# The feed-forward part of a decoder step in two phases: inner features through DRAM, down projection with seven products

## The chip, the cores and the metric

The kernel is one program on one core of a Trainium2 chip. The metric is the device time of that core in microseconds. Three runs of the kernel before took 2767.11, 2770.23 and 2770.42 us; the median is 2770.23 us. All data is float32; the matmuls read float32r operands.

## The reference, cut to what matters

The program is one step of a one-layer hybrid decoder for 512 prompt tokens and 8 sample tokens (520 columns, in two halves of 260). Projections, four mixers and cross attention come first and are not touched. The change lies in the last lines of the layer:

```python
D_MODEL = 2048; D_FF = 4 * D_MODEL

xm = rmsnorm(h, p['norm_mlp_g'])
h = h + jnp.square(jax.nn.relu(xm @ p['w_up'])) @ p['w_down']
...
y = RMSNorm_final(h)
```

## The kernel before, in words

Everything is kept transposed: features on the 128 partitions, the 520 tokens along the columns. Each float32 operand is split into a high part (rounded to float32r) and a low part (the rest), and each product of 128x128 weights by 260 columns is three matmuls: high by high, high by low, low by high. For weights, ScalarE makes the high part `whi` by a copy of 128x1024, and VectorE makes the low part `wlo` by a subtraction. Four slots of each are in use, so a part can be made up to four units ahead of TensorE.

The 8192 inner features are done in 8 chunks of 8 tiles (KF = 8). Chunk 0 takes its up projection as plain tiles (`up_tile`, `up_low`). In that stage VectorE also forms sums of the four quarters of the moving operand (two feature halves by two token halves, `sums_of`, `sums_low` into `th`, `tl`). The other chunks use these sums for a seven-product form of a 2x2 block multiplication (Strassen's, in Winograd's form): a quad is two output tiles of 128 features, computed by seven products of 24 matmuls instead of eight.

A quad needs four pieces of `w_up` (A11, A22, A21, A12, 512 KB each, in the ring RAW4) and sums of them. S1 = A21 + A22 is not made by VectorE: SP loads A21's columns a second time into `sums` and GpSimd issues an adding DMA S1 += A22 (line 947). S2 = S1 - A11, A21 := A11 - A21 and S2 := A12 - S2 are VectorE operations (`sum_of`, k = 2, 3, 4: lines 3058, 3061, 3065). The order by which VectorE works is written out by hand in `quad`. The load of S1 for the next quad waits for the low part of the fifth product, which reads S1:

```python
sp.wait_ge(s.s_sum, 2 * KF + 3 * Q - 2)
sp.wait_ge(s.w_lo, product_of(*((c, q - 1) if q else (c - 1, QUADS - 1)), 4) + 1)
sp.dma_start(S1.rearrange("p (k n) -> p k n", n=P),
             kp(io["w_up"])[:, 0:KF, col:col + P]).then_inc(s.glu_in, 16)
```

Results of the products are combined by VectorE and ScalarE into `c1` and `c2t`, then come relu and square, and the split into `fh` and `fl` (`hidden_even`, `hidden_odd`).

After each chunk's up projection comes its part of the down projection: 16 output tiles of 48 matmuls (`down_part`, line 2259). For each tile VectorE multiplies the PSUM tile by rB, the inverse root mean square (line 3146), and adds it to the residual tile `hr`, which ScalarE's queue loads from `hscr` in DRAM and stores back (line 3150). In the last chunk the sum goes to `hF`, and squares are gathered for the final norm.

Of the kernel before, what the change touches and what calls it, by code (L numbers as in the profile page):

```python
# [21 lines left out]
P = 128  # L22
# [34 lines left out]
U_DOWN = 4 * (T_MLP + QUADS)  # L57
PRODUCTS = 7
U_CHUNK = PRODUCTS * QUADS + KT
SLOT = (0, 1, 2, 3, 0, 1, 3)  # L60

O_KV, O_OUT, O_Q, O_O, O_MLP = 30, 38, 54, 70, 86
O_DOWN = O_MLP + KF


def unit_of(c, n):

    return U_DOWN + U_CHUNK * c + n


def product_of(c, q, s):

    return U_DOWN + KT + U_CHUNK * (c - 1) + PRODUCTS * q + s


def group_of(c, g):

    return g if c == 0 else (QUADS + 4) * c - 4 + g


def quad_of(c, q):

    return QUADS * (c - 1) + q
# [7 lines left out]
HID_ORDER = (range(KF), (1, 0, 3, 2, 5, 4, 7, 6))  # L91
# [80 lines left out]
def build(nc, io, consts_ap, outs):  # L172
# [8 lines left out]
    dscr = nc.dram_tensor("dscr", [128], F32, kind="Internal").ap()  # L181
    hscr = nc.dram_tensor("hscr", [P, KT, TOK], F32, kind="Internal").ap()
# [22 lines left out]
    with ctx:  # L205
# [19 lines left out]
        fh = at("fh", [P, KF, TOK], R_H, F32R)  # L225
        fl = at("fl", [P, KF, TOK], R_H + LO // 2, F32R)
# [4 lines left out]
        hF = at("hF", [P, KT, TOK], R_B)  # L231
        raw2 = at("raw2", [P, 2, 1024], R_A + KT * HALF * 4)
        sums = at("sums", [P, 2, 1024], R_A + LO + KT * HALF * 4)
# [97 lines left out]
        ynat = at("ynat", [P, 5, D], R_A)  # L331
# [53 lines left out]
        part = at("part", [P, TOK], FFN)  # L385
        hr = at("hr", [P, 4, TOK], FFN + 3168)
        msum = at("msum", [P, 2, 2, HALF], FFN + 3168)
        tsum = at("tsum", [P, 4, HALF], FFN + 3168 + 4160)
        rF = at("rF", [P, 8], R_S + 1024)
# [180 lines left out]
        s.hid_hi = sem("hid_hi")  # L570
# [5 lines left out]
        s.h_add = sem("h_add")  # L576
# [29 lines left out]
        def halves(t):  # L606
# [5 lines left out]
        hr_in, HR_IN = (s.h_in, s.kh_in, s.vh_in), (48, 64, 64)  # L612
        hr_st, HR_ST = (s.xs_st, s.ys_st), (64 + 16 * KT, 576)
# [9 lines left out]
                 (mh[:, 1, KF:KT, :], ml[:, 1, KF:KT, :]))  # L623

# [59 lines left out]
        def _(sp):  # L684
# [142 lines left out]
            def load_quad(c, q):  # L827

                for r, (i, j) in enumerate(((0, 0), (1, 1), (1, 0), (0, 1))):
                    if q == 0:  # L830
                        n = unit_of(c - 1, KT - 4 + r)
                        sp.wait_ge(s.w_hi, n + 1)
# [7 lines left out]
                    if r == 2:  # L840
                        Q = quad_of(c, q)
                        if Q > 0:
                            sp.wait_ge(s.s_sum, 2 * KF + 3 * Q - 2)
                            sp.wait_ge(s.w_lo, product_of(*((c, q - 1) if q else (c - 1, QUADS - 1)), 4) + 1)
# [2397 lines left out]
```

## Time and profile before

| | |
|---|---|
| median of 3 runs | 2770.23 us (2767.11 to 2770.42) |
| the profiled execution, whole time | 2766.59 us |
| its span | 2764.8 us |
| TensorE busy | 2731.3 us, 99% |
| VectorE busy | 1513.4 us, 55% |
| ScalarE busy | 910.8 us, 33% |
| GpSimd busy | 618.6 us, 22%, none of it arithmetic in the feed-forward part |
| DMA | 428.92 MB, 155 GB/s over the span |

The busy time of an engine is the union of its instructions' spans. Matmuls overlap in the rows: one is shown with 0.28 us, though one starts each 0.12 us. The time from start to start is what counts for a sum. The same holds for VectorE: an operation of 1024 columns shows 1.22 us, and the next starts 1.14 us after it. The granted clock of TensorE was 0.992 on average.

### The profile page before, as it was taken

To read this page: it belongs to the slowest core of one execution; us is meant where nothing else is said; L and a number is where in the kernel's file an instruction comes from. 1 tells how busy PE (TensorE), PEld (TensorE's weight loads), DVE (VectorE), ACT (ScalarE), POOL (GpSimd) and SP (SyncE) were. 2 spreads that over 40 slices of the span, in tenths; PEclk is the share of its full clock that TensorE was granted. 3 is DMA by queue.
4 is the path that set the end of the run, shared out by engine and by line. 5 is a ranking of instruction groups with operands and counts; after the bars stand their busy time and mean duration, and the time that the engine had idled before them with its cause. 6 is when DMAs were issued, how large, how long until landed. Compare 5 with 4: busy or idle time off the path is not lost.

```text
span 2764.8 us, 51075 instructions
## 1 busy us (share of the span) xinstructions
PE 2731.3 (99%) x21572; PEld 2616.8 (95%) x21572; DVE 1513.4 (55%) x2063; ACT 910.8 (33%) x1187; POOL 618.6 (22%) x292
## 2 busy tenths in 40 slices
PE   9999999999999999999999999999999999999998
PEld 7999998777999988789999999999999999999998
DVE  4687936666323334422474655746557465564665
ACT  5221125535222211222332432514325143251442
POOL 2545434675443322344200000000000000000000
PEclk9999999999999999999999999999999999999999
DMA  6734345555532666543327666666665665656653
GB/s 191 142 101 103 103 129 163 169 176 162 169 91 76 206 198 198 161 133 114 109 83 215 166 173 181 159 187 165 173 180 157 191 162 170 179 157 197 162 143 109
DMA packets 576409, 428.92 MB, mean 155 GB/s; under 512 B 36041, under 2 KB 493615, under 8 KB 574767
## 3 DMA queue, kind: packets, MB, share of 16 engines
q1 hardware_dynamic: 500152, 308.70, 38.8%
q10 hardware_dynamic: 72027, 102.69, 12.3%
q0 software_dynamic: 4032, 14.68, 2.8%
q8 instruction: 149, 2.44, 0.4%
q14 instruction: 49, 0.40, 0.0%
HBM read 357.78 MB, written 53.84 MB: 149 GB/s over the span
## 4 chain that ended last, share of the span: by engine, by line
PE 86%; issue 6%; POOL 4%; DVE 2%; ACT 1%; DMA 1%; SPq 0%; POOLq 0%; DVEq 0%; ACTq 0%
PE lin L1654 32%; PE lin L2259 27%; PE aux L2224 17%; PE lin L2224 3%; POOL wlo L932 3%; POOL wlo L890 2%; PE aux L1976 1%; PE aux L1931 1%; PE lin L1871 1%; PE aux L1922 1%; PE lin L1744 1%; DVE rot L2311 0%; PE aux L1821 0%; PE aux L1817 0%; DMA piece<-in_cache_mem_v 0%
## 5 line engine op out<-in xcount | busy, mean ns | idle before, releaser
L890 POOL TENSOR_TENSOR wlo<-raw,whi 128x1024 fp32r<-128x1024 f32 x176 | 433.6, 2467 | 658.9 <-ACT whi L976 467.3
L2259 PE MATMUL lin<-fl,whi 128*128 128x260 f32 x2048 | 577.3, 282 | 0.0
L2259 PE MATMUL lin<-fh,wlo 128*128 128x260 f32 x2048 | 577.2, 282 | 0.0
L2259 PE MATMUL lin<-fh,whi 128*128 128x260 f32 x2048 | 576.8, 282 | 0.0
L1486 ACT ACTIVATE whi<-raw 128x1024 fp32r<-128x1024 f32 x212 | 224.2, 1057 | 507.6 <-DVE hr L3150 400.1
L2259 PEld LDWEIGHTS lin<-fh,wlo 128*128 128x128 f32 x2048 | 385.8, 188 | 0.0
L2259 PEld LDWEIGHTS lin<-fh,whi 128*128 128x128 f32 x2048 | 385.2, 188 | 0.0
L2259 PEld LDWEIGHTS lin<-fl,whi 128*128 128x128 f32 x2048 | 384.9, 188 | 0.0
L3041 DVE TENSOR_TENSOR wlo<-raw,whi 128x1024 fp32r<-128x1024 f32 x240 | 292.6, 1219 | 29.8 <-ACT whi L1486 29.8
L947 POOL DMA_DIRECT2D sums<-raw x28 | 24.4, 871 | 1242.8 <-DMA sums<-in_w_up 1242.8
L3146 DVE TENSOR_TENSOR part<-lin,rB 128x520 f32<-128x520 f32 x128 | 89.5, 699 | 383.0 <-PE lin L2259 376.5
L976 ACT ACTIVATE whi<-raw 128x1024 fp32r<-128x1024 f32 x140 | 147.7, 1058 | 452.6 <-PE lin L1654 324.9
L1654 PE MATMUL lin<-xh,whi 128*128 128x260 f32 x896 | 257.3, 287 | 0.0
L1654 PE MATMUL lin<-xl,whi 128*128 128x260 f32 x896 | 254.5, 284 | 0.0
L1654 PE MATMUL lin<-xh,wlo 128*128 128x260 f32 x896 | 254.2, 284 | 0.0
L2224 PE MATMUL aux<-th,wlo 128*128 128x260 f32 x672 | 189.8, 282 | 0.0
L2224 PE MATMUL aux<-th,whi 128*128 128x260 f32 x672 | 189.7, 282 | 0.0
L2224 PE MATMUL aux<-mh,wlo 128*128 128x260 f32 x672 | 189.7, 282 | 0.0
L2224 PE MATMUL aux<-ml,whi 128*128 128x260 f32 x672 | 189.7, 282 | 0.0
L2224 PE MATMUL aux<-mh,whi 128*128 128x260 f32 x672 | 189.7, 282 | 0.0
L2224 PE MATMUL aux<-tl,whi 128*128 128x260 f32 x672 | 189.6, 282 | 0.0
L1654 PEld LDWEIGHTS lin<-xh,whi 128*128 128x128 f32 x896 | 170.2, 190 | 2.5 <-issue 1.7
(483 smaller groups left out, 6836.4 us busy)
## 6 DMA issues: line engine op xcount, KB each, us to landing
raw<-in_w_up SPq DMA_DIRECT2D x128, 512.0 KB, 4.4
raw<-in_w_down SPq DMA_DIRECT2D x128, 512.0 KB, 4.3
hr<-hscr ACTq DMA_DIRECT2D x128, 260.0 KB, 3.4
raw<-in_w_in SPq DMA_DIRECT2D x60, 512.0 KB, 3.8
hscr<-hr ACTq DMA_DIRECT2D x112, 260.0 KB, 2.1
raw<-in_w_out SPq DMA_DIRECT2D x32, 512.0 KB, 3.9
raw<-in_w_q SPq DMA_DIRECT2D x32, 512.0 KB, 4.0
piece<-in_cache_mem_k SPq DMA_DIRECT2D x32, 512.0 KB, 6.0
```

The costliest lines, as they stand in the source:

```text
L890: pool.tensor_tensor(wlo[:, slot, :], raw[:, slot % 2, :], whi[:, slot, :].bitcast(F32), ALU.subtract).then_inc(s.w_lo, 1)
L932: pool.tensor_tensor(wlo[:, slot, :], src, whi[:, slot, :].bitcast(F32), ALU.subtract).then_inc(s.w_lo, 1)
L976: act.activation(whi[:, slot, :], raw[:, slot % 2, :], ACT.Copy).then_inc(s.w_hi, 1)
L1486: act.activation(whi[:, slot, :], src, ACT.Copy).then_inc(s.w_hi, 1)
L1654: mm = pe.matmul(lin[:, 2 * i + f, 0:HALF], w, x, start=(n == 0 and part == 0), stop=(n == KT - 1 and part == 2))
L1744: mm = pe.matmul(lin[:, 2 * i + f, 0:HALF], w, m[:, kk, HALF * f:HALF * f + HALF], start=(kk == 0 and part == 0), stop=(kk == KT - 1 and p ...
L1871: mm = pe.matmul(lin[:, 2 * i + f, 0:HALF], w, m[:, k, HALF * f:HALF * f + HALF], start=(k == 0 and part == 0), stop=(k == KT - 1 and part ...
L1922: mm = pe.matmul(aux[32 * j:32 * j + 32, 2, :], pTd[:, m, 32 * b:32 * b + 32], piece[:, j, m, :], start=(g == 0 and m == 0), stop=(g == 1 ...
L2224: mm = pe.matmul(out, w, m[:, kk, :], start=(first and kk == 0 and part == 0), stop=(last and kk == KF - 1 and part == 2), skip_group_chec ...
L2259: mm = pe.matmul(lin[:, 2 * i + f, 0:HALF], w, x[:, kk, HALF * f:HALF * f + HALF], start=(first and m == 0 and part == 0), stop=(last and ...
L3041: v.tensor_tensor(wlo[:, slot, :], src, whi[:, slot, :].bitcast(F32), ALU.subtract).then_inc(s.w_lo, 1)
L3146: v.tensor_tensor(halves(part[:]), lin_tile(n % 2), halves(rB[:]), ALU.mult).then_inc(s.tile_free, 1)
```

## The change

Phase 1 computes the up projection of all eight chunks without a break: four pairs of plain tiles, then 28 quads. rB, which before was applied after the down projection, is applied to the squared features. From each quad of feature tiles (two of an even, two of an odd tile's halves) VectorE forms the four sums that the seven-product form of the down projection wants (`hidden_sums`), and ScalarE's queue stores the seven blocks to a new DRAM tensor `hidd` by two DMAs per quad (`store`).

Phase 2 goes through the chunks again. SP loads a chunk's seven blocks (`load_block`, 532 KB each) into one of two sets, ScalarE and VectorE split each into its high and low part (`block_hi`, `block_lo`). The 16 output tiles of a chunk are 4 groups of 4 tiles; a group is seven products of 24 matmuls, on A11, A22, A21, A12 of `w_down` and four sums, now all made by VectorE (`down_sum`). ScalarE copies the PSUM pair X three times (`copied`), VectorE adds four corners into `cbuf`, and GpSimd's queue adds `cbuf` onto the residual `hscr` in DRAM by an adding DMA, except in the last chunk, where `hscr` is loaded into `hF` and VectorE adds.

```diff
+    hidd = nc.dram_tensor("hidd", [N_CHUNK, P, 7, 4, HALF], F32, kind="Internal").ap()
 # GpSimd's queue
-            for c in range(1, N_CHUNK):
-                for u in range(QUADS):
+            for Q in range(N_QUAD):
...
+            for G in range(N_GROUP - GROUPS):
+                g = G % GROUPS
+                pool.wait_ge(s.c_done, C_DONE + 4 * G + 4)
+                pool.dma_start(hscr[:, 4 * g:4 * g + 4, :], cbuf[G % 2][:], accum_op=ALU.add, max_dma_last_dim=4160).then_inc(c_add[G % 2], 16)
 # ScalarE
-                act.activation(fh[:, tile, :], buf, ACT.Copy).then_inc(s.hid_hi, 1)
+            def store(R):
+                c, kk = R // QUADS, R % QUADS
+                act.wait_ge(s.t_done, T_DONE + R + 1)
+                dma(hidd[c, :, 0, kk, :], st[:, R % 2, 0, :], st_out[R % 2])
+                dma(hidd[c, :, 1:7, kk, :], st[:, R % 2, 2:8, :], st_out[R % 2])
+            def quad(Q):
...
                 for k in (4, 5, 6):
-                    hi_product(c, q, k)
+                    hi_up(Q, k)
+                store(QUADS + Q - 1)
 # TensorE
-            down(0, HID_ORDER[0])
-            for c in range(1, N_CHUNK):
-                for u in range(QUADS):
-                    quad(c, u)
-                down(c, HID_ORDER[1])
+            def down_product(G, k, first, last):
+                n, p = down_n(G, k), G // GROUPS
+                pe.wait_ge(s.w_lo, n + 1)
+                if G % GROUPS == 0:
+                    pe.wait_ge(s.blk_lo, BLK_LO + 7 * p + k + 1)
+                hi, lo = xbh[p % 2][k], xbl[p % 2][k]
+                for pr in range(2):
+                    for kk in range(4):
...
+            def group(G):
+                if G > 0:
+                    pe.wait_ge(s.copied, COPIED + 3 * G)
+                down_product(G, 0, True, True)
+                if G > 0:
+                    pe.wait_ge(s.c_done, C_DONE + 4 * G)
...
+                down_product(G, 1, True, True)
...
+            for Q in range(N_QUAD):
+                quad(Q)
+            for G in range(N_GROUP):
+                group(G)
 # VectorE
+            def hidden_sums(R):
+                b = st[:, R % 2, :, :]
+                tt(b[:, 4:6, :], b[:, 1:4:2, :], b[:, 0:2, :], ALU.subtract)
+                tt(b[:, 6, :], b[:, 3, :], b[:, 4, :], ALU.subtract)
+                tt(b[:, 7, :], b[:, 6, :], b[:, 2, :], ALU.subtract, s.t_done)
+            def even(Q):
+                v.wait_ge(s.up_sq, act_n(Q, 6))
+                v.tensor_tensor(st[:, Q % 2, 0:2, :], halves(c1[:]), halves(rB[:]), ALU.mult).then_inc(s.hid_lo, 1)
+                v.wait_ge(s.hid_lo, KF + 2 * Q + 2)
+                hidden_sums(QUADS + Q)
...
             for p in range(QUADS):
...
+                if p == 0:
+                    inverse(6, D, 2)
+                up_scaled(p, 0)
...
-                if p == 0:
-                    inverse(6, D, 2)
...
+                v.wait_ge(s.hid_lo, 2 * p + 2)
+                hidden_sums(p)
+            up_sum(0, 2)
+            for Q in range(N_QUAD):
+                quad(Q)
+                if Q == N_QUAD - 2:
+                    block_lo(0)
+                    block_lo(1)
```

The order on VectorE in the middle of a quad, before: from S2 (`sums<-sums,raw`) to the low part of the fifth product (the third `wlo<-sums` or, counted with raw, the fourth `wlo` row here). `raw` is A11 or A22, `raw_68` is A21 or A12.

```order
L3058 TENSOR_TENSOR sums<-sums,raw 128x1024
L3074 TENSOR_TENSOR fl<-c2t,fh 128x520
L3041 TENSOR_TENSOR wlo<-raw,whi 128x1024
L3061 TENSOR_TENSOR raw_68<-raw,raw_68 128x1024
L3041 TENSOR_TENSOR wlo<-sums,whi 128x1024
L3082 TENSOR_TENSOR c_199<-u_203,aux 128x260
L3041 TENSOR_TENSOR wlo<-raw_68,whi 128x1024
L3070 TENSOR_TENSOR fl<-c_199,fh 128x520
L3041 TENSOR_TENSOR wlo<-sums,whi 128x1024
```

And the same stretch now, where `raw_66` is A21 or A12 and `st` is the staging buffer of the blocks:

```order
L3165 TENSOR_TENSOR sums<-sums,raw 128x1024
L3203 TENSOR_TENSOR st<-c2t,rB 128x520
L3150 TENSOR_TENSOR wlo<-raw,whi 128x1024
L3168 TENSOR_TENSOR raw_66<-raw,raw_66 128x1024
L3150 TENSOR_TENSOR wlo<-sums,whi 128x1024
L3208 TENSOR_TENSOR c_233<-u_237,aux 128x260
L3150 TENSOR_TENSOR wlo<-raw_66,whi 128x1024
L3195 TENSOR_TENSOR st<-c_233,rB 128x520
L2406 TENSOR_TENSOR st<-st 128x520
L2406 TENSOR_TENSOR st<-st 128x260 x2
L3150 TENSOR_TENSOR wlo<-sums,whi 128x1024
```

The two splits into `fl` are now multiplications into `st`, and two more rows (three operations) stand before the last row, the low part that the load of the next S1 waits for.

The order on VectorE in the down projection, before, two tiles of 16:

```order
L3041 TENSOR_TENSOR wlo<-raw_68,whi 128x1024
L3146 TENSOR_TENSOR part<-lin,rB 128x520
L3150 TENSOR_TENSOR hr<-hr,part 128x520
L3041 TENSOR_TENSOR wlo<-raw_68,whi 128x1024
L3146 TENSOR_TENSOR part<-lin,rB 128x520
L3150 TENSOR_TENSOR hr<-hr,part 128x520
```

And now, from the second corner of a group (`u3d,lin`) over the group's end to its fourth corner (`u2d,lin`), which frees the PSUM pair that the second product of the next group writes:

```order
L3259 TENSOR_TENSOR cbuf_97<-u3d,lin 128x2x260
L3150 TENSOR_TENSOR wlo<-raw,whi 128x1024
L3180 TENSOR_TENSOR sums<-raw_66,raw 128x1024
L3261 TENSOR_TENSOR cbuf_97<-u3d,aux 128x2x260
L3184 TENSOR_TENSOR sums<-sums,raw 128x1024
L3150 TENSOR_TENSOR wlo<-sums,whi 128x1024
L3186 TENSOR_TENSOR raw_66<-raw,raw_66 128x1024
L3263 TENSOR_TENSOR cbuf_97<-u2d,lin 128x2x260
```

Where two operations on a PSUM tile followed one low part, six operations, three of them sums of weights, now stand between the second corner and the fourth.

## Rows read from the trace of the kernel before

**Rows 1.** The page, parts 1 and 4: busy us and share, and the last chain.
```profile
PE 2731.3 (99%) x21572; PEld 2616.8 (95%) x21572; DVE 1513.4 (55%) x2063; ACT 910.8 (33%) x1187; POOL 618.6 (22%) x292
PE 86%; issue 6%; POOL 4%; DVE 2%; ACT 1%; DMA 1%; SPq 0%; POOLq 0%; DVEq 0%; ACTq 0%
```
**Rows 2.** The chain in order of time: start us, us, what; two down stages.
```profile
1447.24 91.69 PE lin L2259 x768
...
2651.41 91.68 PE lin L2259 x768
```
**Rows 3.** Busy us by engine, clock, DMA share and GB/s, of three stages.
```profile
1366.90:1447.24 80.34, 80.34 (x675) 80.34 (x674) 61.62 (x83) 30.10 (x35) 0.00 (x0) 1.00 0.27 79
1619.29:1710.96 91.67, 91.67 (x771) 91.67 (x770) 40.21 (x48) 17.50 (x18) 0.86 (x1) 1.00 0.64 188
1710.96:1791.31 80.35, 80.35 (x674) 80.35 (x674) 60.62 (x68) 44.08 (x58) 2.58 (x3) 1.00 0.60 155
```
**Rows 4.** VectorE's timeline in quads: start us, us, operation, idle before it.
```profile
1712.35 1.22 DVE L3058 TENSOR_TENSOR sums<-sums,raw 128x1024 f32<-128x1024 f32 x1
...
1730.16 1.23 DVE L3058 TENSOR_TENSOR sums<-sums,raw 128x1024 f32<-128x1024 f32 x1 [2.44 <-DMA sums<-raw]
1731.30 0.69 DVE L3074 TENSOR_TENSOR fl<-c2t,fh 128x520 fp32r<-128x520 f32 x1
1731.91 1.22 DVE L3041 TENSOR_TENSOR wlo<-raw,whi 128x1024 fp32r<-128x1024 f32 x1
...
1738.79 1.23 DVE L3041 TENSOR_TENSOR wlo<-sums,whi 128x1024 fp32r<-128x1024 f32 x1 [0.52 <-ACT whi L1501]
...
1749.35 1.23 DVE L3058 TENSOR_TENSOR sums<-sums,raw 128x1024 f32<-128x1024 f32 x1 [1.55 <-DMA sums<-raw]
...
1769.33 1.23 DVE L3058 TENSOR_TENSOR sums<-sums,raw 128x1024 f32<-128x1024 f32 x1 [1.45 <-DMA sums<-raw]
```
**Rows 5.** SP's load of S1 and GpSimd's adding DMA of the same quad.
```profile
1740.09 0.37 SPq L845 DMA_DIRECT2D sums<-in_w_up  x1
1744.58 0.85 POOL L947 DMA_DIRECT2D sums<-raw  x1 [18.18 <-DMA sums<-in_w_up]
```
**Rows 6.** A dependent pair of 260 columns on VectorE; and ScalarE's square.
```profile
1742.56 0.43 DVE L3102 TENSOR_TENSOR u<-u,lin 128x260 f32<-128x260 f32 x1
1743.02 0.42 DVE L3104 TENSOR_TENSOR c2t<-u,aux 128x260 f32<-128x260 f32 x1
...
1736.22 0.64 ACT L1506 ACTIVATE c<-c 128x520 f32<-128x520 f32 x1
```
**Rows 7.** The page, part 3: queues of ScalarE (q10) and GpSimd (q0).
```profile
q10 hardware_dynamic: 72027, 102.69, 12.3%
q0 software_dynamic: 4032, 14.68, 2.8%
```
**Rows 8.** DMA in windows 1744.5:1749.4, then 1869:1877; last, all 28 adding DMAs.
```profile
sums<-raw POOLq DMA_DIRECT2D x1, 512.0 KB, 4.7
...
q10 hardware_dynamic: 286, 0.52, 18.7%
...
sums<-raw POOLq DMA_DIRECT2D x1, 512.0 KB, 7.0
...
DMA to landing us min/median/max: 4.5/5.2/7.2
```
**Rows 9.** The chain in the tail, between VectorE's last sum and TensorE.
```profile
2746.64 0.14 issue
```
**Rows 10.** ScalarE's square of the last plain tile; VectorE's reciprocal in the first.
```profile
1448.07 0.64 ACT L1595 ACTIVATE hsqF<-upr 128x520 f32<-128x520 f32 x1 [3.88 <-DVE upr L3017]
...
1382.02 3.40 DVE L2329 RECIPROCAL rB<-rB 128x520 f32<-128x520 f32 x1
```
**Rows 11.** ScalarE's groups in 1620:2650: busy us, mean ns of one, idle before.
```profile
L1501 ACT ACTIVATE whi<-sums 128x1024 fp32r<-128x1024 f32 x72 | 76.2, 1058 | 180.2 <-DVE sums L3058 88.4 <-PE lin L2224 83.0 <-DVE sums L3065 8.8
...
L1532 ACT ACTIVATE p<-aux 128x260 f32<-128x260 f32 x24 | 8.9, 370 | 0.0
```

More of the change, by code:

```diff
@@ L575, in build @@
         s.q_ev = sem("q_ev")
-        s.h_add = sem("h_add")
+        s.c_add0 = sem("c_add0")
+        s.c_add1 = sem("c_add1")
         s.f_ev = sem("f_ev")
@@ new lines, in group @@
+            def group(G):
+                p, g = G // GROUPS, G % GROUPS
+                blocks = [7 * (p + 1) + k for k in ((0,), (1, 2), (3, 4), (5, 6))[g]] if p + 1 < N_CHUNK else []
+                end = p == N_CHUNK - 1
+                hi_down(G, 2)
+                if G == 0:
+                    block_hi(5)
+                    even(N_QUAD - 1)
+                if end:
+                    load_last(g)
+                copied(G, 0, p1d)
+                hi_down(G, 3)
+                if G == 0:
+                    block_hi(6)
+                if G == 1:
+                    store(QUADS + N_QUAD - 1)
+                if end and g > 0:
+                    last_half(2 * g - 2)
+                hi_down(G, 4)
+                for j in blocks[0:1]:
+                    block_hi(j)
+                copied(G, 2, u2d)
+                hi_down(G, 5)
+                for j in blocks[1:2]:
+                    block_hi(j)
+                if end and g > 0:
+                    last_half(2 * g - 1)
+                hi_down(G, 6)
+                copied(G, 4, u3d)
+                if G + 1 < N_GROUP:
+                    hi_down(G + 1, 0)
+                    hi_down(G + 1, 1)
@@ L2265, in down @@
[L2265 to L2278 removed]
+                product(up_n(Q, 6), *MOVES[6], BANK_B, False, True)
@@ new lines, in down_product @@
+            def down_product(G, k, first, last):
+                n, p = down_n(G, k), G // GROUPS
+                pe.wait_ge(s.w_lo, n + 1)
+                if G % GROUPS == 0:
[3 more added lines that the diff above has]
+                    for kk in range(4):
+                        wh = whi[:, n % 4, 256 * kk + P * pr:256 * kk + P * pr + P]
+                        wl = wlo[:, n % 4, 256 * kk + P * pr:256 * kk + P * pr + P]
+                        for part, (w, m) in enumerate(((wh, hi), (wh, lo), (wl, hi))):
+                            mm = pe.matmul(DOWN_BANK[k][:, pr, :], w, m[:, kk, :], start=(first and kk == 0 and part == 0),
+                                           stop=(last and kk == 3 and part == 2), skip_group_check=True)
+                mm.then_inc(s.pe_unit, 1)
@@ L3096, in quad, with corner @@
+            def corner(Q):
+                v.wait_ge(s.pe_unit, up_n(Q, 6) + 1)
+                v.tensor_tensor(c1[:, HALF:TOK], u2[:], BANK_B, ALU.add).then_inc(s.q_ev, 1)
+            def quad(Q):
+                up_sum(Q, 3)
+                lo_up(Q, 2)
+                if Q > 0:
+                    corner(Q - 1)
+                lo_up(Q, 3)
+                if Q > 0:
+                    even(Q - 1)
+                lo_up(Q, 4)
+                v.wait_ge(s.pe_unit, up_n(Q, 2) + 1)
                 v.wait_ge(s.up_sq, act_n(Q, 1))
```

669 lines of the change are left out of this document (363 added, 306 removed).

## Prediction, made before the changed kernel had run

> **What bounds the kernel now.** I read the page's busy shares first. TensorE is busy 99% of the span, VectorE 55% and ScalarE 33%, and the chain that ended last is 86% TensorE [rows 1]. The ordered chain then shows the feed-forward part as an unbroken run of TensorE from 1447.24 to 2743 us: every 768 matmuls of the down projection, one chunk's, take 91.7 us [rows 2]. Four quads take 80.35 us, and TensorE is busy for all of both stages [rows 3]. That is 91.67/768 = 0.1194 us a matmul, 24 x 0.1194 = 2.87 us a product, and 20.09 us a quad of seven products. The granted clock there is 1.00, its upper level, so no share of the time is a lowered clock [rows 3]. Removed matmuls are therefore worth their full pitch, but only while every operand of a product is ready each 2.87 us. So the second question is how much room the feeding engines have.
>
> For that I read VectorE's timeline over one quad, with the SP and GpSimd rows beside it. There a 1024-column operation takes 1.14 us from start to start and one of 520 takes 0.61 [rows 4]. One loop feeds the next quad, and it runs through DMA. The sum S2 of quad Q starts at T0 = 1730.16. VectorE's queue reaches the fifth product's low part (wlo) at 1738.79 (T0 + 8.63). SP waits for it and issues the load of S1 at 1740.09. GpSimd issues the adding DMA S1 += A22 at 1744.58, and the next S2 starts at 1749.35, idle until that DMA landed [rows 4, 5]. The loop took 19.19 us there and 19.98 the next time. TensorE needs 20.09. The loop has half a microsecond of room, and today it never runs more than four quads before 91.67 us of down projection let it catch up.
>
> **The change, part by part.** (1) TensorE. The down projection had 128 tiles of 48 matmuls = 6144. It becomes 32 groups of 7 x 24 = 5376. The 768 that go are exactly one piece of the chain: -91.7 us. The up projection's count stays, 28 quads of 168. Shapes stay 128x128 by 260 columns, so I keep the pitch.
>
> (2) The loop in the quads. VectorE's `hidden_even` and `hidden_odd` (one 520-column operation each, 0.70 us) become a multiplication by rB each, the same size; ScalarE's copies to fh go. `even` then adds three dependent operations in front of the fifth wlo, one of 520 and two of 260 columns. A dependent operation starts 0.03 us after the end of the one before it: 0.46 us from start to start for 260 columns [rows 6], 0.73 for 520. So with the multiplication 0.73 + 0.73 + 0.46 + 0.46 = 2.38 us. The multiplication waits for the square, which ends at 1736.86, not for the fh copy after it, and starts at about 1736.88. The fifth wlo then starts at 1739.26 where it was 1738.79: +0.47. The loop becomes 19.66 us, or about 20.06 on the mean of its two instances.
>
> (3) The store of the sums to `hidd`. ScalarE issues it behind its whi copy of the seventh product. That copy waits for a sum which VectorE starts at 9.10 + 1.14 + 0.4 + 1.14 = T0 + 11.8 (two low parts and a 260-column operation after the fifth) and ends 1.2 later; with the copy's 1.06 the store is issued at T0 + 14.1. The adding DMA is issued at 10.40 + 4.49 = T0 + 14.9. They run together. The store is 128 x 7 x 1040 B = 0.93 MB. ScalarE's queue moved 102.69 MB in 12.3% of 2765 us of all sixteen engines, so the store wants 3.1 us of them [rows 7]. What company costs the add is seen in two windows: with SP's load alone beside it, it landed 4.7 us after issue; with 0.52 MB of q10 traffic as well it took 7.0 [rows 8]. All 28 lie between 4.5 and 7.2. Bounds for the delay: nothing (the store started earlier and moves aside), and 2.3 x 0.93/0.52 = 4.1 us. I take 1.5 us: about a third of the store's work is done before the add starts, and the 7.0 is near the longest of the 28. The loop is then 19.66 + 1.5 = 21.2 us, and 0.1 for TensorE's restart (0.14 us stand between VectorE's end and the matmul in the tail [rows 9]) makes 21.3: 1.2 us over 20.09. The up phase is now 28 quads in a row with nothing to catch up in, so 26 turns x 1.2 = +31 us. TensorE will wait at the second product of each quad, whose wlo ends T0 + 3.0.
>
> (4) Start of the up phase. Today the first down tiles lie between the plain up tiles and quad 0; now quad 0 follows at once. After TensorE's last plain tile come relu on VectorE and the square on ScalarE, to 1448.71 [rows 10], then the multiplication and the three sums (2.38), then S2 (1.14), the next sum with ScalarE's whi behind S2's end (1.06), and wlo (1.22). The third product's operand is ready at 1454.7, 7.4 us after quad 0's start, and needed at 5.74: +1.8 with the restart. S2 of quad 1 then comes 17.4 us (the first loop of a chunk took 17.8 from 1712.35 to 1730.16 [rows 4], less 0.4 because no feature tile is due in it) and 1 us for the store later, another +0.6. Together +2.4. The 3.40 us reciprocal moves forward inside the first plain tile [rows 10]; that stage has 61.6 busy us of VectorE in 80.34 [rows 3] and wlo two units ahead, so I cost it, and the sums there (1.65 x 4), at nothing. If the cover is gone it is 3 us once.
>
> (5) From up to down. Two block splits of 1040 columns (1.16 us each) are put before the third product of quad 27: 2.3 less 0.6 of lead, +1.7. Behind quad 27's fifth product VectorE has wlo, split, sum, split, multiplication, sum and wlo before the corner that product 1 of group 0 waits for, and two of the splits wait for ScalarE, which first takes the corner of product 5. From the end of product 5: 0.75 for that corner on ScalarE, 1.1 for the block's copy, then 1.2 + 1.14 + 1.16 + 0.61 + 1.14 + 1.14 + 0.45 on VectorE = 8.7, where TensorE arrives after 2 x 2.87 = 5.7: +3.0. Split, sum and wlo behind it make product 2 wait 0.6. Split, multiplication with its sums (1.16 + 2.38) and wlo make product 3 wait 1.9, and sum, split and wlo hold product 4 for 0.6: +6 in all.
>
> (6) A down group. VectorE's work is 7 wlo and 4 sums of 1024 (1.14 each from start to start), 4 corners of 520 (0.61) and 1.75 splits (1.16): 12.5 + 2.4 + 2.0 = 17.0 us of 20.06, so it fits. But one chain does not. From the end of a group's fifth product: ScalarE's copy of 520 PSUM columns 0.6 (260 take 0.37, 520 from SBUF 0.64), whi 1.06 [rows 11], then on VectorE wlo, sum, corner, sum, wlo, sum, corner = 5 x 1.14 + 0.62 + 0.70, with 0.15 of event times: 8.8 us. TensorE reaches the second product of the next group, which needs that last corner's bank, after 3 x 2.87 = 8.6. With the restart it is 0.3 a group, 28 times: +8 or 9. In the last pass an addition onto the residual (1.16) joins it three times: +4. Together +13.
>
> (7) DMA in the down phase. Weights 2.1 MB, blocks 0.93 MB and the addition 1.06 MB in 20 us make 204 GB/s; the down stage of before moved 188 GB/s at a share of 0.64 [rows 3]. The additions are nowhere in the trace with a DRAM destination. From the nearest row, 0.52 MB in 2.8% of the span over 28 is 2.8 us [rows 7], they take 5.6 us; twice that still ends before `cbuf` is wanted two groups later. I take 0, bounds 0 and 30 us (one more microsecond on the A22 load in each group; that load has 1.2 us of room). Removed: 128 loads and 112 stores of hr, which were hidden; 0.
>
> (8) The tail. The last add and square are 1040 columns instead of 520, and ScalarE scales two tiles (0.64 each) before its table load: +1.5.
>
> Sum: -91.7 + 31 + 2.4 + 1.7 + 6 + 13 + 1.5 = -36.1. The profiled execution had 2764.8 us of span and 2766.59 in all; the median shown is 2770.23. On the execution's own 2766.6 that makes 2730.5, on the median, 3.6 higher, 2734. I forecast 2734.
>
> A rule of the Trainium skill bears on (3). Its page DMA: Bandwidth & Descriptors, section Queues, rings and completion order, says that an engine goes round its queues packet by packet and takes some 9 to 17 descriptors from one before it turns to the next. By it the add's nine packets per engine would wait behind one such turn of the store's 56. That is an estimate of 0.5 to 0.9 us out of 3.1, and the sum by it would be 2708 to 2718. The 7.0 us landing in company speaks for more, with half the bytes.
>
> **Rivals.** A: the loop stays hidden. The store starts 0.8 us before the add and may be mostly through, or delay it by 0.5 us. For it: a loop of 19.19 was seen, and the median of the 28 landings, 5.2, is only 0.5 above 4.7 although SP's load runs beside them [rows 8]. Against: the 7.0. The excess falls to 0.1 to 0.4 us and (3) to about 6: 2709. The rule of the skill above leads here too. B, slower than before: the add lands as late as bytes in company suggest. Place: the wait of S2 in each quad. Price: 4.1 us, loop 23.8, 26 x 3.8 = 99 in place of 31: 2803. It decides from the point where a quad takes 22.6 us, since 26 x 2.5 = 65 and the 25 of the other parts use up the 91.7. C: the down phase is what suffers, because additions to DRAM are slow and hold up A22: +30 on the forecast, 2765. D: the products are in place but TensorE's pitch changes with the new access; nothing in the rows speaks for it, all forms at L2259 and L2224 have 282 ns.
>
> **Chances.** Forecast (2715 to 2755) 0.45; A 0.28; C and what lies between 2755 and the old time 0.15; B 0.12. Differences under 0.2%, 5.5 us, can't be told from none: C's end reaches into that, 0.05. So faster 0.83, same 0.05, slower 0.12. The range 2698 to 2772 leaves out B and the best corner of A.
>
> **What will show it.** TensorE should have some 20,810 matmuls (21,572 less 768, and a few in the last sums) at 282 ns. The wait of S2 for `sums<-raw` should grow from 38.6 us in 21 waits, quads should take 21.3 us in the ordered chain (20.09 under A, over 22.6 under B), and TensorE should idle for a wlo on sums or raw in them. Down groups should take 20.3 to 20.4 us with the wait on a corner. The forecast is wrong if down groups exceed 21 us, if quads keep 20.1, or if the matmul pitch differs from 0.1194.

## The result, and the profile after

The changed kernel took 2816.6 us (median; 2811.9 to 2821.5), the kernel before 2770.3 us beside it. The ratio is 1.017, 95% interval 1.015 to 1.019: slower by 46 us, where 36 us less was forecast.

The page of the changed kernel, whose profiled execution took 2821.5 us: the span, the busy times and the chain that ended last, as in [rows 1].

```profile
span 2819.6 us, 50173 instructions
PE 2685.0 (95%) x20814; PEld 2556.9 (91%) x20814; DVE 1787.7 (63%) x2293; ACT 1079.7 (38%) x1379; POOL 650.8 (23%) x320
PE 44%; DVE 20%; issue 14%; DMA 14%; POOL 5%; ACT 3%; SPq 0%; POOLq 0%; ACTq 0%; DVEq 0%
```

The matmuls went as they should (21,572 to 20,814). But TensorE is now 44% of the last chain where it was 86%. VectorE, DMA and issue times hold most of the rest: TensorE waits.

The windows of the feed-forward part of the changed kernel, first up to the wait in quad 27, then the down groups; below them 500 us from within each. Columns as in [rows 3].

```profile
1451.25:2077.81 626.56, 570.17 (x4562) 564.52 (x4560) 443.71 (x542) 273.47 (x353) 23.28 (x27) 0.97 0.67 180
2077.81:2793.20 715.39, 675.73 (x5522) 668.54 (x5523) 583.37 (x569) 352.08 (x405) 33.81 (x28) 0.99 0.68 185
...
1500.00:2000.00 500.00, 457.81 (x3674) 453.38 (x3673) 359.89 (x440) 220.48 (x286) 18.96 (x22) 0.97 0.66 179
2150.00:2650.00 500.00, 474.01 (x3901) 469.19 (x3902) 402.87 (x391) 241.36 (x274) 28.98 (x24) 1.00 0.72 191
```

The kernel before had no idle time in these stages. Here TensorE idles 56.4 us in the first window (626.56 - 570.17) and 39.7 in the second. Its busy time is also longer than its matmuls at 0.1194 us want: by 25.5 us in the first (570.17 - 4562 x 0.1194) and by 16.4 in the second. Part of that is each last matmul before a wait, shown with its whole 0.28 us; the rest is a lowered clock. So the up part lost 81.9 us and the down part 56.1, together 138. Less the 91.7 us of the removed matmuls that is +46. The two profiled spans differ by 54.8: the feed-forward part also began 4.0 us later, and what follows it took 4.7 us more (step 8 below). From the 500 us windows a quad takes 168 x 500/3674 = 22.9 us (20.09 before), a down group 168 x 500/3901 = 21.5.

One quad of the changed kernel, which answers to [rows 4, 5]: VectorE, the store's two DMAs on ScalarE's queue, SP's load, GpSimd's adding DMA, and TensorE's wait at the second product of the next quad. Columns: start us, us, what, idle before it.

```profile
1727.93 1.23 DVE L3165 TENSOR_TENSOR sums<-sums,raw 128x1024 f32<-128x1024 f32 x1 [5.67 <-issue]
...
1737.07 1.23 DVE L3150 TENSOR_TENSOR wlo<-sums,whi 128x1024 fp32r<-128x1024 f32 x1
...
1750.54 1.23 DVE L3165 TENSOR_TENSOR sums<-sums,raw 128x1024 f32<-128x1024 f32 x1 [5.81 <-issue]
```
```profile
1740.94 1.01 ACTq L1035 DMA_DIRECT2D hidd<-st  x2
```
```profile
1738.37 0.37 SPq L865 DMA_DIRECT2D sums<-in_w_up  x1
```
```profile
1742.77 0.86 POOL L998 DMA_DIRECT2D sums<-raw  x1 [21.71 <-DMA sums<-in_w_up]
```
```profile
1753.57 0.54 PE L2307 MATMUL aux<-th,whi 128*128 128x260 f32 x1 [2.25 <-DVE wlo L3150]
```

T0 is again the start of S2, here 1727.93. The fifth low part starts at T0 + 9.14, S1 is asked for at T0 + 10.44, and the adding DMA is issued 4.40 us later, at T0 + 14.84. Up to there all is as forecast. From that issue to the next S2 it takes 7.77 us, where [rows 4, 5] have 4.77. VectorE idles 5.81 us ahead of it. The row gives "issue" as releaser, that is, the profile shows no event for this wait, so it has to be read from the adding DMA's issue and landing.

The store is asked for at T0 + 13.01, 1.83 us ahead of the adding DMA. The DMA in the window 1740.9:1742.7, between the two issues: q10, ScalarE's queue, is not among its queues.

```profile
q1 hardware_dynamic: 595, 0.30, 56.9%
```

By the packet records of the trace the store's first packet moves after the adding DMA's issue in each of the 26 full quads, by 0.2 to 1.0 us.

What moved in the 4.2 us behind the issue, and in the 4 us after that: DMA queues of the changed kernel in windows 1742.7:1746.9 and 1747:1751 (packets, MB, share of the engines), and the landing times of all 28 adding DMAs.

```profile
q10 hardware_dynamic: 827, 0.84, 58.4%
q1 hardware_dynamic: 950, 0.48, 40.4%
q0 software_dynamic: 3, 0.01, 1.5%
```
```profile
q0 software_dynamic: 140, 0.51, 64.1%
```
```profile
DMA to landing us min/median/max: 4.7/7.8/10.0
```

For 4.2 us the adding DMA (q0) moved 3 of its 144 packets, while ScalarE's store (q10) moved 827 and SP's load of A12 (q1) 950. Only then did its other packets move. (The store counts 928 here, 896 rows of 1040 bytes and 32 small ones.) The median of the 28 landings went from 5.2 [rows 8] to 7.8.

In the down part, the chain of the changed kernel from the sixth product's high part to the corner that frees TensorE's bank at 2300.45, in order of time (start us, us, what):

```profile
2285.89 1.06 ACT whi L1541
...
2286.97 1.24 DVE wlo L3150
...
2288.27 6.26 DMA raw<-in_w_down
...
2294.55 1.23 DVE sums L3180
2295.78 0.06 DVE cbuf L3261
...
2296.30 1.22 DVE sums L3184
2297.52 1.14 DVE wlo L3150
2298.66 1.13 DVE raw L3186
2299.79 0.62 DVE cbuf L3263
```

Two links stand in it. The A22 load takes 6.26 us, and the first sum of the next group waits for it. Then that sum and four more operations on VectorE stand ahead of the fourth corner, which frees TensorE's bank (of the third corner, L3261, the chain shows 0.06 us). Page part 6 of the changed kernel gives the loads' median, and that of the additions in DRAM:

```profile
raw<-in_w_down SPq DMA_DIRECT2D x128, 512.0 KB, 7.0
...
hscr<-cbuf POOLq DMA_DIRECT2D x28, 1040.0 KB, 10.6
```

How the addition holds the load is seen in two windows of the same group. The addition is issued at 2279.70, two `w_down` loads at 2282.70 and 2283.89, A22's at 2288.27. First 2282.5:2287, then 2288.2:2294.6:

```profile
q0 software_dynamic: 177, 0.74, 92.1%
q1 hardware_dynamic: 14, 0.01, 1.1%
...
raw<-in_w_down SPq DMA_DIRECT2D x2, 512.0 KB, 8.8
```
```profile
q1 hardware_dynamic: 1624, 2.15, 98.7%
q0 software_dynamic: 22, 0.07, 5.2%
```

In the first the addition has the engines and SP's queue moves next to nothing, with two loads waiting. In the second SP's queue moves four times the bytes of one load, and the addition is all but over. So A22 stands behind the loads that the addition had held, and not beside the addition.

### The profile page after: what moved, and what is told of

It reads as the page before. It is cut to its first block, busy times and chain, and to the rows that moved or that the text cites. A ratio compares the mean times of both kernels' runs of the same rounds, so it can differ in the third digit from the quotient of the medians.

```text
span 2819.6 us, 50173 instructions
## 1 busy us (share of the span) xinstructions
PE 2685.0 (95%) x20814; PEld 2556.9 (91%) x20814; DVE 1787.7 (63%) x2293; ACT 1079.7 (38%) x1379; POOL 650.8 (23%) x320
## 4 chain that ended last, share of the span: by engine, by line
PE 44%; DVE 20%; issue 14%; DMA 14%; POOL 5%; ACT 3%; SPq 0%; POOLq 0%; ACTq 0%; DVEq 0%
PE lin L1738 28%; PE lin L2342 7%; DMA raw<-in_w_down 7%; DVE wlo L3150 6%; DMA sums<-in_w_up 4%; POOL wlo L984 3%; DMA sums<-raw 2%; POOL wlo L942 2%; DVE st L2406 2%; DVE sums L3180 1%; DVE sums L3184 1%; DVE raw L3186 1%; ACT whi L1541 1%; DVE raw L3168 1%; PE aux L2060 1%
## 5 line engine op out<-in xcount | busy, mean ns | idle before, releaser
L2342 PE MATMUL lin<-xbh,whi 128*128 128x260 f32 x1280 | 366.6, 286 | 38.8 <-DVE cbuf L3263 35.8
L2342 PE MATMUL lin<-xbl,whi 128*128 128x260 f32 x1280 | 363.1, 284 | 0.0
L2342 PE MATMUL lin<-xbh,wlo 128*128 128x260 f32 x1280 | 363.0, 284 | 0.0
L1541 ACT ACTIVATE whi<-sums 128x1024 fp32r<-128x1024 f32 x180 | 190.4, 1058 | 400.6 <-DVE sums L3165 146.4
L1032 ACT ACTIVATE whi<-raw 128x1024 fp32r<-128x1024 f32 x140 | 147.4, 1058 | 452.4 <-PE lin L1738 313.1
L2342 PEld LDWEIGHTS lin<-xbh,whi 128*128 128x128 f32 x1280 | 242.3, 189 | 45.7 <-DVE cbuf L3263 42.5
L1541 ACT ACTIVATE whi<-raw 128x1024 fp32r<-128x1024 f32 x240 | 249.7, 1052 | 56.4 <-DVE raw L3168 51.5
L2307 PE MATMUL aux<-th,whi 128*128 128x260 f32 x672 | 202.2, 301 | 56.4 <-DVE wlo L3150 56.4
L2342 PEld LDWEIGHTS lin<-xbh,wlo 128*128 128x128 f32 x1280 | 242.6, 189 | 0.0
L2342 PEld LDWEIGHTS lin<-xbl,whi 128*128 128x128 f32 x1280 | 242.4, 189 | 0.0
L3150 DVE TENSOR_TENSOR wlo<-sums,whi 128x1024 fp32r<-128x1024 f32 x180 | 219.7, 1220 | 7.8 <-ACT whi L1541 5.9
L2307 PEld LDWEIGHTS aux<-th,whi 128*128 128x128 f32 x672 | 135.8, 202 | 62.2 <-DVE wlo L3150 62.0
## 6 DMA issues: line engine op xcount, KB each, us to landing
hscr<-cbuf POOLq DMA_DIRECT2D x28, 1040.0 KB, 10.6
```

Source lines behind the costliest of these rows:

```text
L1032: act.activation(whi[:, slot, :], raw[:, slot % 2, :], ACT.Copy).then_inc(s.w_hi, 1)
L1541: act.activation(whi[:, n % 4, :], src, ACT.Copy).then_inc(s.w_hi, 1)
L2307: mm = pe.matmul(out, w, m[:, kk, :], start=(first and kk == 0 and part == 0), stop=(last and kk == KF - 1 and part == 2), skip_group_chec ...
L2342: mm = pe.matmul(DOWN_BANK[k][:, pr, :], w, m[:, kk, :], start=(first and kk == 0 and part == 0), stop=(last and kk == 3 and part == 2), s ...
L3150: v.tensor_tensor(wlo[:, n % 4, :], src, whi[:, n % 4, :].bitcast(F32), ALU.subtract).then_inc(s.w_lo, 1)
```

## The experiments

All start from the changed kernel; each ratio is to the kernel before, with its 95% interval.

**The store in the up phase.** First, the store moved from behind the seventh high part to the quad's end:

```diff
                 for k in (4, 5, 6):
                     hi_up(Q, k)
-                store(QUADS + Q - 1)
...
                 act.activation(c1[:, 0:HALF], BANK_A, ACT.Relu).then_inc(s.up_sq, 1)
+                store(QUADS + Q - 1)
```

> ScalarE issues a quad's store of the hidden sums at the end of the quad (about T0 + 17.6) and no longer at T0 + 13.4. Theory 1, the store's packets hold back the adding DMA: the add's first packet then comes about 1.4 us after its issue and its last some 4.7 us after, the loop falls from 23.0 to about 20.1 us, the 62 us of waits in the up phase and the lowered clock behind them (18 us) go, 2735 to 2745 us. Theory 2, the loop is long because of VectorE's three sums ahead of the fifth wlo: the loop stays above 22 us and the time within 10 us of 2816.

Measured: 2744.4 us, 0.990 (0.988 to 0.992), 72 us less than the changed kernel. Its windows and landings:

```profile
1500.00:2000.00 500.00, 500.00 (x4183) 499.86 (x4181) 404.13 (x494) 249.50 (x325) 21.55 (x25) 1.00 0.77 206
```
```profile
DMA to landing us min/median/max: 4.5/4.7/8.3
```

The same bytes in the same quads, more of them per second (206 GB/s for 179), and in this window the idle time and the lowered clock are gone. So it was neither the amount nor the bandwidth, but what stood in front of the adding DMA. Theory 1 holds.

By the packet records the add's first packet now comes 1.4 us after its issue (median), where it had been 4.1.

Second, the three sums put behind the fifth low part, the store's place kept:

```diff
+                if Q > 0:
+                    v.wait_ge(s.hid_lo, KF + 2 * Q)
+                    hidden_sums(QUADS + Q - 1)   # now behind lo_up(Q, 4), taken out of even(Q - 1)
```

> The three sums of the hidden features stand behind the fifth wlo on VectorE, not ahead of it; the store stays where it is. Theory 2: the loop loses the whole excess and the time falls by 60 us or more. Theory 1: S1's load is asked for 1.65 us earlier, the loop shortens by 1.65 us at most (and by more only if the add now starts ahead of the store), so the time falls by 26 x 1.65 = 43 us and what the clock gives back, to 2760 to 2775; the add's first packet still comes over 2.5 us after its issue.

Measured: 2811.3 us, 1.015 (1.013 to 1.017): 5 us less. A miss for both theories' sizes. In the same 500 us S1 was asked for 1.2 us earlier (median T0 + 9.26 for T0 + 10.44), and most of that was eaten: the add was issued only 0.7 us earlier, and its median landing was 8.2 us where the changed kernel has 7.8.

```profile
sums<-raw POOLq DMA_DIRECT2D x22, 512.0 KB, 8.2
```

A quad took 168 x 500/3710 = 22.6 us for 22.9. The earlier issue hardly helped a DMA whose landing the store's end sets. The run is not clean: the store waits for the sums, and its second DMA went out half a microsecond later too (median T0 + 13.92 for T0 + 13.44). Theory 2 had 60 us or more for this edit, and with the first run it falls.

Third, only the small one of the store's two DMAs left in place, the large one at the quad's end:

```diff
-                store(QUADS + Q - 1)
+                store(QUADS + Q - 1, True)   # block 0 alone; the six others at the quad's end
```

> Of the store's two DMAs the small one (one block of seven, 128 packets of 1040 B) stays where the change put it and the large one (six blocks, 768 packets) goes to the end of the quad. If the add's start is held back in proportion to the packets queued ahead of it (theory S1), its first packet comes 1.4 + 2.75/7 = 1.8 us after its issue, the loop takes 20.3 to 20.6 us and the time is within 10 us of the 2744 of the kernel that moved both. If any store in that place holds the add back by its own latency (theory S2), the first packet still comes after 4 us, the loop takes over 22 us and the time stays above 2795.

Measured: 2754.5 us, 0.993 (0.991 to 0.995), 10 us above the late store, just at the edge of what theory S1 allowed. Its windows and landings in 1500:2000:

```profile
1500.00:2000.00 500.00, 496.76 (x4138) 495.08 (x4137) 400.06 (x493) 244.19 (x321) 21.55 (x25) 1.00 0.75 203
```
```profile
sums<-raw POOLq DMA_DIRECT2D x25, 512.0 KB, 4.9
```

168 x 500/4138 = 20.3 us a quad. The landing is 0.2 us over the 4.7 of the store moved as a whole, against 3.1 over it with all seven blocks ahead. The delay grows with the packets ahead of the add (theory S1); a store as such costs little.

Fourth, the adding DMA taken away and the store left at T0 + 13.4:

```diff
-                load_first_sum(Q)
-                pool.dma_start(S1, A22, accum_op=ALU.add).then_inc(s.s1_add, 16)
+                    v.tensor_tensor(S1, A21, A22, ALU.add).then_inc(s.s1_add, 1)
```

> VectorE forms S1 = A21 + A22 itself (one more sum of 1024 columns, 1.14 us, in each quad); the second load of A21 into S1 and the adding DMA in SBUF are gone; the store stays where the change put it, at T0 + 13.4. If the store costs time only through the adding DMA (theory 1), the loop through DMA no longer exists, a quad takes 20.1 to 20.4 us although the store is where it was, and the time is 2735 to 2750 us. If the store or VectorE's own load holds the quads up in another way (VectorE would be busy some 18.5 to 19 of 20.1 us), a quad stays above 21 us, over 2775 us.

Measured: 2741.8 us, 0.990 (0.989 to 0.992). Its windows:

```profile
1500.00:2000.00 500.00, 500.00 (x4184) 500.00 (x4183) 439.54 (x521) 254.22 (x323) 0.00 (x0) 1.00 0.54 154
```

With the store where the change put it, TensorE never waits in these quads and VectorE's 88% is still no bound. This edit also takes a 0.5 MB load and the add's own bytes away, so by itself it could be a matter of amount; the first run, which keeps every byte, rules that out. Together they say that the store costs time only through the adding DMA behind it.

**The down groups.** The last corner put ahead of a low part and a sum:

```diff
                     down_sum(G + 1, 2)
+                    corner_of(G, 3)
                     lo_down(G + 1, 1)
...
                 down_sum(G, 3)
-                if G > 0:
-                    corner_of(G - 1, 3)
```

> In a down group VectorE writes the last corner right behind the second sum and ahead of a low part and the third sum. If the chain on VectorE sets the group (theory D1), a group falls from 21.8 to about 20.6 us and the time by 25 to 35 us, to about 2785. If the late A22 load sets it and the next product's low part waits anyway (theory D2), the wait only moves from the corner to that low part and the time falls by under 10 us.

Measured: 2777.2 us, 1.003 (1.002 to 1.004), 39 us less, where 25 to 35 were expected. And the addition in DRAM cut to the first of a group's four tiles (the kernel leaves three quarters of the sum out):

```diff
-                pool.dma_start(hscr[:, 4 * g:4 * g + 4, :], cbuf[G % 2][:], accum_op=ALU.add, max_dma_last_dim=4160)
+                pool.dma_start(hscr[:, 4 * g:4 * g + 1, :], cbuf[G % 2][:, 0:1, :], accum_op=ALU.add)
```

> Only the first of a group's four output tiles is added to the residual in DRAM, the other three are left out, so that the addition moves a quarter of its bytes. If the adding DMA to DRAM is what makes the A22 load land after 6.3 to 7.5 us (theory D3), it lands after 4.4 us, a group takes 20.1 to 20.5 us and the time falls by 35 to 45 us, to about 2775. If it is not, the load keeps over 6 us and the time stays within 6 us of 2816.

Measured: 2788.4 us, 1.007 (1.005 to 1.008), 28 us less, where 35 to 45 were expected, though landing and group came out as expected. The additions that are left also have rows of 2080 bytes in place of 4160, so their amount and the size of their packets changed together. The down windows of the two, and after each the median of its `w_down` loads:

```profile
2150.00:2650.00 500.00, 500.00 (x4175) 500.00 (x4174) 432.62 (x417) 258.15 (x293) 30.16 (x25) 1.00 0.74 203
```
```profile
raw<-in_w_down SPq DMA_DIRECT2D x128, 512.0 KB, 6.4
```
```profile
2150.00:2650.00 500.00, 499.29 (x4114) 494.25 (x4113) 423.11 (x410) 253.44 (x289) 20.96 (x24) 1.00 0.56 163
```
```profile
raw<-in_w_down SPq DMA_DIRECT2D x128, 512.0 KB, 4.5
```

With a quarter of the addition the loads land in 4.5 us and a group takes 168 x 500/4114 = 20.4 us. With the corner early it takes 20.1 us although the loads still need 6.4. Both theories are right: the late load and the order on VectorE are links of one chain, 21.5 - 20.1 = 1.4 us too long. The faster load takes all but 0.3 us of that away, the corner ahead of two operations (1.13 and 1.14 us in the chain above) all of it.

ScalarE's sixth high part ahead of a bank copy, to ask for A22 earlier:

```diff
-                copied(G, 2, u2d)
                 hi_down(G, 5)
+                copied(G, 2, u2d)
```

> In a down group ScalarE makes the sixth product's high part ahead of the copy of the third product's bank, so its low part and the A22 load behind it start 1 us earlier. If the late landing of A22 sets the chain (theory D3), the corner comes 0.5 to 1 us earlier, the time falls by 15 to 28 us, to about 2795. If the order on VectorE alone sets it (theory D1), or the load simply lands as late in the company of the addition, under 6 us.

Measured: 2817.9 us, 1.017 (1.015 to 1.019): nothing. VectorE's first sum still idled for the load, and the median load took 8.4 us where it had taken 7.0:

```profile
L3180 DVE TENSOR_TENSOR sums<-raw,raw 128x1024 f32<-128x1024 f32 x23 | 28.2, 1225 | 22.1 <-DMA raw<-in_w_down 22.1
```
```profile
raw<-in_w_down SPq DMA_DIRECT2D x128, 512.0 KB, 8.4
```

As in the up phase, a load asked for earlier into a busy queue lands no earlier. This run does not say which of the transfers holds it; the quarter of the addition does, by its 4.5, together with the two windows above.

**Together.** The diffs of the late store and of the early corner in one kernel:

> Store at the end of the quad and the last corner ahead of a low part and a sum, together. If the two places are independent, their gains add: 72 + 39 = 111 us, 2705. If one of them had hidden a wait of the other (the clock included), over 2720.

Measured: 2705.5 us, 0.977 (0.975 to 0.978). The two gains (72 and 39 us) add to within a microsecond, so the two places are independent. With the diffs of the later sums and of the earlier high part as well:

> Both edits, and with them the hidden sums behind the fifth low part (loop of 20.2 us less 1.2 = 19.0, below TensorE's 20.1) and the high part of the sixth product ahead of the bank copy. The 13.6 us of waits left in the up phase and most of the 8.5 us in the down phase go: 2685 to 2700. If the pairs of waits that are left have another cause (the step from up to down, the first quad), it stays within 5 us of the kernel with two edits.

Measured: 2708.4 us, 0.977 (0.976 to 0.979): no gain over the last. The adding DMA's median landing is 5.6 us here, where it is 4.7 with the late store alone; that its earlier issue brings it closer to the other transfers is likely and not shown. The expectation missed.

With the diffs of S1 on VectorE, of the late store and of the early corner:

> The same sum on VectorE with the store at the quad's end and the early corner. The kernel with those two edits alone has 10 us of waits and 8 us of lowered clock in the up phase, most of them in quads where the add lands after 6 us. If that add is their cause, 2693 to 2700 us; if they come from the first quad and the step from up to down, 2703 to 2707.

Measured: 2701.6 us, 0.976 (0.975 to 0.978). Its interval overlaps that of the same kernel with the adding DMA, so the 4 us are likely and not shown, and the time lies between the two ranges of the expectation. The 10 us of waits that it starts from are not in the trace of the kernel with the two edits: TensorE waits there twice in the quads, 3.6 us together (in the first quad and in quad 27), and here once, 3.0 us. What stays beside that are 5.7 us at the step from up to down, and waits of at most 0.5 us in the last groups.

For these, `even` of the last quad was put behind the first group's fifth low part (on the kernel with store late and corner early):

```diff
                 if G == 0:
                     block_lo(5)
-                    even(N_QUAD - 1)
...
                 lo_down(G, 4)
+                if G == 0:
+                    even(N_QUAD - 1)
```

> Store late and corner early, and in the first down group the last quad's multiplication and three sums (2.4 us of VectorE) stand behind the fifth product's low part, not ahead of the fourth's. Step 5 of the prediction says they cost a wait there: the waits of 3.2 and 2.8 us at 2027 and 2053 fall by 2 us together, and the clock that is lowered behind them for some 10 us gives 1 to 3 us more: 2700 to 2704. If the waits there come from the two splits of the blocks or from the load of the first group's tiles, no more than 1 us.

Measured: 2706.3 us, 0.976 (0.975 to 0.978): no gain in the median. Two of the five runs took 2696 and 2698 us, below all four of the kernel without this edit (2704 to 2710); the mean granted clock was 0.993 and 0.992 in them and 0.987 to 0.989 in the other three. So a small gain by way of the clock is open. TensorE's idle time at the products after the step moved rather than went; the groups of 2018 to 2075, first with `even` in its old place, then later:

```profile
L2342 PE MATMUL lin<-xbh,whi 128*128 128x260 f32 x90 | 27.7, 308 | 5.7 <-DVE c L3208 3.1 <-DVE wlo L3150 2.6
```
```profile
L2342 PE MATMUL lin<-xbh,whi 128*128 128x260 f32 x97 | 27.8, 286 | 5.3 <-DVE c L3208 3.1 <-DVE wlo L3150 1.9 <-issue 0.3
L2342 PE MATMUL aux<-xbh,whi 128*128 128x260 f32 x40 | 11.4, 285 | 1.5 <-DVE wlo L3150 1.5
```

The 3.1 us belong to a corner of quad 27 (`c`, behind the splits); they are the same in both. The second profile is of the run of 2698 us: it has more idle time (6.8 us for 5.7) and matmuls of 286 in place of 308 ns, that is, less of the lowered clock. The diffs of S1 on VectorE, of the late store, of the early corner and of the later `even`, all together:

> All of these together: store late, corner early, S1 on VectorE, the last sums later. If the gains add, 2690 to 2698 us; if VectorE, busy 19 us of a quad's 20.1, becomes the bound, quads lengthen beyond 20.2 us and it is no faster than the kernel without S1 on VectorE.

Measured: 2698.7 us, 0.974 (0.973 to 0.975), the lowest median of all, though its interval overlaps that of the kernel without the later `even`: 71 us below the kernel before, 118 below the changed one, and just above the expected 2690 to 2698. VectorE is not the bound: 500 us of quads hold 4184 matmuls here too. A window of its groups:

```profile
2150.00:2650.00 500.00, 499.19 (x4164) 498.83 (x4163) 433.12 (x418) 262.06 (x300) 27.98 (x23) 1.00 0.73 199
```

## Why the prediction was wrong

**Step 1, right.** 768 matmuls at 0.1194 us are worth 91.7: where nothing waits, 500 us hold 4184 matmuls of the new kernels, 0.1195 each. The rival of another pitch falls.

**Step 2, right.** Forecast: S1 asked for at T0 + 10.40, the add issued at T0 + 14.9. Measured: 10.44 and 14.84.

**Step 3, the one that failed.** "I take 1.5 us", with bounds of 0 and 4.1. The adding DMA was late by 7.8 - 4.7 = 3.1 us by the medians with and without the store ahead of it. The nearest row [rows 8] gave 2.3 us for 0.52 MB in company, 4.1 for the store's bytes, and I went below both, on the argument that "about a third of the store's work is done before the add starts". The store did go out early, 1.83 us ahead of the add and not the forecast 0.8, but none of its packets had moved when the add was issued. And I had the two sharing the engines; the rows show that the store's packets, and the load's, went first and the add's after them: 830 to 892 of the store's 928 had started before the add's fourth. With 3.1 in place of 1.5 the loop of 21.3 is 22.9, as measured. That is rival B's mechanism, past its decision point of 22.6 us. The sum also started from the shorter of the two loops that it had read (19.19, not the mean of 19.6); up to the add's issue that was right.

**A term that no step had: the clock.** After a wait TensorE often ran slower. Three windows of the changed kernel, before, just behind and after the wait of 2.25 us at 1753.57:

```profile
1749.50:1753.50 4.00, 1.81 (x16) 1.61 (x14) 2.96 (x4) 1.06 (x1) 0.00 (x0) 1.00 0.03 5
1753.60:1757.00 3.40, 3.40 (x16) 3.40 (x17) 3.40 (x4) 1.87 (x3) 0.00 (x0) 0.51 0.21 53
1757.10:1760.50 3.40, 3.40 (x31) 3.40 (x29) 3.24 (x6) 2.31 (x4) 0.00 (x0) 1.00 1.17 313
```

The clock stands at 0.51, its lower level of 1.2 GHz, for 3.40 us, and 16 matmuls start where 31 should. It did not fall after every wait: the trace has 14 such stretches in the feed-forward part, for a wait in each of 27 quads and in most of the 32 groups. In the first 500 us window TensorE idles 42.2 us and its busy time is 457.81 - 3674 x 0.1194 = 19.1 us too long; the ends of 22 last matmuls, 0.16 us each, are 3.5 of these, the clock some 15. So the clock is about a quarter of the up part's 81.9 us, for which steps 3, 4 and the first part of 5 had 35. "No share of the time is a lowered clock" was true of the trace before, in which TensorE never waited there.

**Step 4, right where a row shows it.** The first quad's wait was put at 1.8 us; the row has 1.79:

```profile
1458.94 0.39 PE L2307 MATMUL aux<-th,whi 128*128 128x260 f32 x1 [1.79 <-DVE wlo L3150]
```

In 1366.90:1451.20 TensorE is busy for all of 84.30 us, so the reciprocal and the plain tiles' sums cost nothing, as said. The 0.6 us for quad 1 are not seen apart from the loop.

**Step 5, the places right, the sizes not.** TensorE's waits in quad 27 and at product 1 of group 0, in the changed kernel:

```profile
2077.81 0.52 PE L2307 MATMUL aux<-th,whi 128*128 128x260 f32 x1 [4.41 <-DVE wlo L3150]
2102.37 0.58 PE L2342 MATMUL lin<-xbh,whi 128*128 128x260 f32 x1 [2.48 <-DVE c L3208]
```

The 4.41 us fit the splits' forecast 1.7 and the wait of the loop, 1 to 3 us as in the quads ahead (28 waits, 56.4 us in all); the 2.48, forecast 3.0, is on the corner that the step named. Behind it group 0 waited 0.9 and 0.3 us more, 3.7 in all, where the step had 6. That the last `even` costs 1.9 us there is not borne out: moving it left the idle time as long.

**Step 6, right.** A chain 0.3 us too long, 20.4 us a group. With the loads landing in 4.5 us, near the 4.3 of the kernel before, a group takes 20.4.

**Step 7, the second that failed.** "I take 0, bounds 0 and 30 us." The loads of `w_down` need 7.0 us at the median where the page before has 4.3, so the A22 load, with "1.2 us of room", came late. Groups took 21.5 and not 20.4: 32 x 1.1 = 35 us, and the down part lost 56.1 where the rest of step 5 and step 6 had 19. I computed that the bytes fit (204 GB/s) and not how long a single load would stand behind them. This is rival C's mechanism, and near its price of 30. So B and C came together; the range took in C alone and left B out.

**Step 8, small.** From the last matmul of the groups to the end of the span it is 26.4 us where it was 21.7, +4.7 for a forecast of 1.5. The small matmuls of the final norm in the chain of either kernel, before and after:

```profile
2746.77 1.16 PE lin L2285 x10
```
```profile
2799.02 3.73 PE lin L2378 x20
```

From the groups' last matmul to the first of these it is 5.8 us for 3.7, that is 2.1 more for the forecast 1.5. The other 2.6 are the small matmuls, 20 in place of 10 and at a granted clock of 0.50 (2798.8:2803) in place of 1.00 (2746:2750); the step had neither. The 4.0 us by which the feed-forward part began later say nothing: the programs are alike ahead of it, and its first matmul came between 1444.6 and 1454.2 us in kernels that differ only behind it.

With the measured sizes in the same sum: -91.7 + 81.9 + 56.1 = +46.3 for the feed-forward part, and with 4.0 and 4.7 the two profiled spans differ by 54.8. The medians differ by 46.3. That this equals the feed-forward part is chance: the profiled execution of the changed kernel was the slowest of its four, that of the kernel before was faster than its others.

## What to carry to other kernels

A DMA that closes a loop between engines must not be issued behind a bulk transfer that nobody waits for: move the bulk transfer in time, not the critical one, and look at the landing time of the critical DMA, not at the share of the bandwidth. When a kernel whose TensorE never waits is brought to wait a little and often, count what the clock takes after each wait as well. Between two bounds of an unshown delay take the value that the nearest row gives. And an early issue is not a head start: look in the rows for when the first packet moves.

## What the runs showed of the hardware

- The adding DMA had moved 3 of 144 packets 4.1 us after its issue, behind a store of 928 packets and a load. One seventh of that store ahead of it made it land 0.2 us later, all of it 3.1 us. By the Trainium skill (page DMA: Bandwidth & Descriptors, section Queues, rings and completion order) an engine turns from queue to queue after typically some 9 to 17 descriptors, with a ceiling of 64. The typical turn would have let the add in after a first turn of the store, and my estimate from it was 0.5 to 0.9 us. This case does not agree with it: by medians the delay was 3.1 us, about the store's own 3.1 us of engine time. The store's 56 an engine lie under the ceiling, so that part of the rule is not contradicted here.
- In the down part it was the other way round: for 4.5 us an addition to DRAM had 92.1% of the engines and SP's queue moved 14 packets, with two loads issued into it.
- A DMA's issue is not its start: the store's first packet moved 2.4 us after its issue in the quad shown (1743.33 for 1740.94), the add's 1.4 us after its own with no store ahead.
- Asking for a transfer earlier gained nothing where its queue or engines were full: 1.2 us earlier in the quads gave 5 us in 28 quads (the store moved by 0.5 us with it), and the earlier sixth high part gave nothing, with loads of 8.4 us in place of 7.0.
- An adding DMA to DRAM of 1.06 MB took 10.6 us; with a quarter of it the median 0.5 MB load of `w_down` fell from 7.0 to 4.5 us.
- A wait of 2.25 us was followed by a stretch at a granted clock of 0.51, in which 16 matmuls started where 31 start at 1.00. The windows of kernels without waits in the quads have 1.00 throughout.
